# Another order for the paired projection: last two products exchanged, bank sums reordered, row buffers swapped by pair, with row stores, an evacuation and 32 narrow columns moved

## What is computed

```python
def mlstm_project(h, w_in, b_in):
    p = h @ w_in + b_in
    q, k, v, o, gates = jnp.split(p, [hk, 2 * hk, 2 * hk + hv, 2 * hk + 2 * hv], axis=-1)
    ...
# then, per chunk of 128 tokens and in both directions:
#   C_new = a * C + einsum(ws, k, v);  h = (w_inter * q @ C + s @ v) / max(|den|, exp(-m))
```

## Time and profile before

| what | value |
|---|---|
| median of 3 runs | 2076.72 us (2072.17 to 2077.28) |
| profiled execution, its own time | 2077.57 us |
| its span, first to last instruction | 2075.5 us |
| mean granted clock of TensorE | 0.981 of full speed |
| busy: TensorE, its weight loads | 2004.3, 1655.5 us |
| busy: VectorE, GpSimd, ScalarE | 1311.3, 1042.5, 843.7 us |

### The profile page before, as it was taken

The page is one execution under the profiler, slowest core; times in us unless marked ns, Lnnn a source line. Parts: engine busy times, 40 slices in busy tenths (PEclk is TensorE's granted clock), DMA queues, the critical chain, the costliest instruction groups (busy, mean ns, idle before and its releaser), DMA issues.

```text
span 2075.5 us, 24059 instructions
## 1 busy us (share of the span) xinstructions
PE 2004.3 (97%) x9095; PEld 1655.5 (80%) x9095; DVE 1311.3 (63%) x1378; ACT 843.7 (41%) x1118; POOL 1042.5 (50%) x610
## 2 busy tenths in 40 slices
PE   6999999999999999998999999988999999999999
PEld 5788888888788888786787888766788888878877
DVE  6889998877648774975424565589655555523125
ACT  5433356465443222322245464445344334412135
POOL 1376755555212222133474446648877877722254
PEclk7999999999999999999999999999999999999999
DMA  9641112222117543433354765341222222253123
GB/s 377 205 153 41 54 46 74 56 74 70 45 61 267 196 136 89 161 116 100 119 178 142 258 229 163 92 152 61 61 61 62 79 83 86 68 192 125 45 89 127
DMA packets 267920, 248.79 MB, mean 120 GB/s; under 512 B 8266, under 2 KB 229203, under 8 KB 267811
## 3 DMA queue, kind: packets, MB, share of 16 engines
q1 hardware_dynamic: 252243, 229.51, 34.8%
q10 hardware_dynamic: 15568, 17.83, 2.4%
HBM read 203.46 MB, written 43.84 MB: 119 GB/s over the span
## 4 chain that ended last, share of the span: by engine, by line
PE 52%; issue 11%; POOL 6%; DVE 3%; DMA 2%; ACT 1%; SPq 0%; POOLq 0%; DVEq 0%; ACTq 0%
PE PS L2412 16%; PE PS L1902 12%; PE PS L2205 6%; PE PS L2304 5%; PE PS L2175 4%; POOL wl L930 3%; PE PS L2426 1%; PE PS L2248 1%; PE PS L2249 1%; PE PS L2257 1%; PE PS L1932 1%; POOL SCR L1148 1%; PE PS L2091 1%; PE PS L2338 1%; POOL wl L1135 1%
## 5 line engine op out<-in xcount | busy, mean ns | idle before, releaser
L930 POOL TENSOR_TENSOR wl<-raw,wh 128x1024 fp32r<-128x1024 f32 (+1 forms) x145 | 351.2, 2423 | 731.9 <-ACT wh L1204 511.8
L1902 PE MATMUL PS<-XH,wh 128*128 128x512 f32 x1232 | 382.6, 392 | 5.8 <-DVE XL L3263 1.8
L1902 PE MATMUL PS<-XH,wl 128*128 128x512 f32 x1232 | 381.6, 391 | 0.0
L1902 PE MATMUL PS<-XL,wh 128*128 128x512 f32 x1232 | 381.0, 390 | 0.0
L1902 PEld LDWEIGHTS PS<-XH,wh 128*128 128x128 f32 x1232 | 229.3, 188 | 55.1 <-issue 3.0
L1204 ACT ACTIVATE wh<-raw 128x1024 fp32r<-128x1024 f32 (+1 forms) x96 | 98.3, 1024 | 425.0 <-PE PS L1902 141.9
L1902 PEld LDWEIGHTS PS<-XL,wh 128*128 128x128 f32 x1232 | 230.1, 188 | 46.9
L1902 PEld LDWEIGHTS PS<-XH,wl 128*128 128x128 f32 x1232 | 229.8, 188 | 46.6
L2655 DVE SCALAR_TENSOR_TENSOR PS<-B,PJ,PS 128x1022 f32<-128x1022 f32 (+7 forms) x197 | 251.1, 1274 | 7.5
L1277 ACT ACTIVATE wh<-raw 128x1024 fp32r<-128x1024 f32 x48 | 50.8, 1058 | 248.0 <-PE PS L1902 228.6
L1135 POOL TENSOR_TENSOR wl<-SCR,wh 128x512 fp32r<-128x512 f32 x80 | 114.2, 1428 | 69.8 <-ACT wh L1730 69.4
(11 more groups left out here) (487 smaller groups left out, 4252.2 us busy)
## 6 DMA issues: line engine op xcount, KB each, us to landing
raw<-in_ffn_up_w SPq DMA_DIRECT2D x48, 512.0 KB, 4.1
raw<-in_w_in SPq DMA_DIRECT2D x40, 512.0 KB, 4.7
raw<-in_m_in_w SPq DMA_DIRECT2D x37, 512.0 KB, 4.2
SCR<-in_ada_w SPq DMA_DIRECT2D x32, 512.0 KB, 6.7
mod_tiles<-in_mod_w SPq DMA_DIRECT2D x16, 512.0 KB, 13.2
B<-in_ada_w SPq DMA_DIRECT2D x16, 512.0 KB, 4.7
raw<-in_w_out SPq DMA_DIRECT2D x16, 512.0 KB, 4.7
raw<-in_m_out_w SPq DMA_DIRECT2D x16, 512.0 KB, 4.2
```

The source lines that it names most:

```text
L930: tt(wl[slot][:, 0:kc, :], raw[slot][:, 0:kc, :], wh[slot][:, 0:kc, :].bitcast(F32), ALU.subtract).then_inc(lo_done, 1)
L1902: last = mm(ps[:, c:c + step_n], W[:, k, :], Y[:, k, c:c + step_n], start=(seen == 0), stop=(seen == total - 1))
```

## The change

The last two products of each pair are exchanged: products run in the order 0, 1, 2, 3, 4, 6, 5. The seven bank sums follow in the order 1, 4, 3, 6, 3, 2, 5, so that row v is complete after the sixth and row g after the seventh; ScalarE finishes v first and g second. The row buffers change roles from pair to pair. All seven sums of the last pair are made before the recurrence's first key weighting, and TensorE waits for all seven before the first state update. The gate rows are stored after the load of unit 9 instead of unit 7, and SyncE waits for their landing only before it reads them back. VectorE evacuates pass 2 of the value projection before the t3 sums instead of after them. The 32 narrow columns of G2 follow one each behind each wide product instead of two behind each pair.

```diff
@@ o_place, o_out @@
+        O_ORDER = (0, 1, 2, 3, 4, 6, 5)
+        O_SUMS = (1, 4, 3, 6, 3, 2, 5)
+
+        def o_place(q):
+            s, n = divmod(q, 7)
+            return s, O_ORDER[n]
+
-        def o_out(i):
+        def o_out(s, i):
-            return stage[i // 2][:, CTX + HALF * (i % 2):CTX + HALF * (i % 2 + 1)]
+            return stage[(i // 2 + s) % 2][:, CTX + HALF * (i % 2):CTX + HALF * (i % 2 + 1)]
@@ SyncE @@
                 if u in (6, 10, 14):
                     v_store((u - 6) // 4)
-                if u == 7:
+                if u == 9:
                     rows_store()
-                    sp.wait_ge(*at("rows_out", 16 * 10))
...
             for s in range(O_PAIRS):
                 pair_load(s + 1)
                 if s == COLS_AT - 1:
+                    sp.wait_ge(*at("rows_out", 16 * 10))
@@ GpSimd @@
             def o_low(q):
                 pool.wait_ge(*at("oq_hi", q + 1))
-                tt(ring(wl, q), o_weights(q % 7), ring(wh, q).bitcast(F32), ALU.subtract).then_inc(ev("oq_lo"), 1)
+                tt(ring(wl, q), o_weights(o_place(q)[1]), ring(wh, q).bitcast(F32), ALU.subtract).then_inc(ev("oq_lo"), 1)
...
-                pool.wait_ge(*at("oq_lo", 7 * s - 3 + n))
+                if s:
+                    pool.wait_ge(*at("oq_lo", 7 * (s - 1) + O_ORDER.index(3 + n) + 1))
@@ ScalarE @@
             def o_high(q):
-                s, i = divmod(q, 7)
+                s, i = o_place(q)
...
             def o_finish(s, v):
 
-                act.wait_ge(*at("osum_ok", SUMS * s + (4, 7)[v]))
-                row = stage[v][:, CTX:ALL]
+                act.wait_ge(*at("osum_ok", SUMS * s + (7, 6)[v]))
+                row = stage[(v + s) % 2][:, CTX:ALL]
...
-                act.dma_start(...).then_inc(ev(f"proj_out{v}"), 16)
+                act.dma_start(...).then_inc(ev(f"proj_out{(v + s) % 2}"), 16)
...
                 o_copy(s)
                 if s:
-                    o_finish(s - 1, 1)
+                    o_finish(s - 1, 0)
                 o_high(7 * s + 5)
                 o_high(7 * s + 6)
                 if s < O_PAIRS - 1:
-                    for i in range(3):
+                    for i in range(4):
                         o_high(7 * (s + 1) + i)
-                    o_finish(s, 0)
-                    o_high(7 * (s + 1) + 3)
+                    o_finish(s, 1)
...
+            o_finish(O_PAIRS - 1, 1)
             o_finish(O_PAIRS - 1, 0)
-            o_finish(O_PAIRS - 1, 1)
@@ TensorE @@
                         for c in range(0, n, step_n):
                             last = mm(ps[:, c:c + step_n], W[:, k, :], Y[:, k, c:c + step_n], start=(seen == 0), stop=(seen == total - 1))
+                            if single and seen < total - 1:
+                                single(2 * seen + c // step_n)
...
             def late_columns(step_n):
-                if step_n == 6:
+                c = step_n - 10
+                if c == 0:
                     pe.wait_ge(*at("late_summed", LATE * KD))
-                for c in range(max(2 * step_n - 12, 0), min(2 * step_n - 10, LATE * KD)):
+                if 0 <= c < LATE * KD:
                     ins = mm(LATE_PS[:, c:c + 1], late_acc[:, c * P:(c + 1) * P], ones[:], start=True, stop=True)
...
-            group(G2, release="x_used_G2", opened=True, narrow=late_columns)
+            group(G2, release="x_used_G2", opened=True, single=late_columns)
...
             def o_product(s, i):
-                q, (W_H, W_L) = 7 * s + i, (ring(wh, 7 * s + i), ring(wl, 7 * s + i))
-                X_H, X_L = o_tokens(i)
+                q = 7 * s + O_ORDER.index(i)
+                (W_H, W_L), (X_H, X_L) = (ring(wh, q), ring(wl, q)), o_tokens(i)
...
-                    before, n = divmod(earlier[-1], 7)
-                    if n == 0:
+                    before, j = o_place(earlier[-1])
+                    if j == 0:
                         pe.wait_ge(*at("opair_copy", before + 1))
                     else:
-                        pe.wait_ge(*at("osum_ok", SUMS * before + (0, 1, 7, 6, 2, 4, 5)[n]))
+                        pe.wait_ge(*at("osum_ok", SUMS * (before + 1) - O_SUMS[::-1].index(j)))
...
-                for i in range(7):
+                for i in O_ORDER:
                     o_product(s, i)
...
                     if y:
                         pe.wait_ge(*at("p_ok", y))
-                    else:
-                        pe.wait_ge(*at("osum_ok", SUMS * O_PAIRS))
...
                     if x == 0 and h == 0:
-                        pe.wait_ge(*at("osum_ok", SUMS * (O_PAIRS - 1) + 5))
+                        pe.wait_ge(*at("osum_ok", SUMS * O_PAIRS))
@@ VectorE @@
             def bank_sum_pair(s, n):
-                i = (1, 4, 3, 5, 6, 3, 2)[n]
-                dve.wait_ge(*at("oq_used", 7 * s + max(i, (1, 4, 4, 5, 6, 6, 6)[n]) + 1))
+                i = O_SUMS[n]
+                dve.wait_ge(*at("oq_used", 7 * s + max(O_ORDER.index(j) for j in O_SUMS[:n + 1]) + 1))
                 if n == 0:
                     dve.wait_ge(*at("opair_copy", s + 1))
-                    dve.wait_ge(*at("proj_out0", 16 * (DIRECT[0] + s)))
+                    dve.wait_ge(*at(f"proj_out{s % 2}", 16 * (DIRECT[s % 2] + s)))
                 else:
-                    dve.wait_ge(*at("osum_ok", SUMS * s + (0, 1, 2, 3, 3, 5, 5)[n]))
-                if n == 5:
-                    dve.wait_ge(*at("proj_out1", 16 * (DIRECT[1] + s)))
-                g0, g1, v0, v1, u = o_out(0), o_out(1), o_out(2), o_out(3), US[:]
-                dst, src = ((g0, u), (u, u), (g1, u), (g1, g1), (u, u), (v1, u), (v0, u))[n]
-                V.tensor_tensor(dst, o_bank(7 * s + i), src, ALU.add).then_inc(ev("osum_ok"), 1)
+                    dve.wait_ge(*at("osum_ok", SUMS * s + (0, 1, 2, 3, 4, 4, 6)[n]))
+                if n == 4:
+                    dve.wait_ge(*at(f"proj_out{1 - s % 2}", 16 * (DIRECT[1 - s % 2] + s)))
+                g0, g1, v0, v1, u = o_out(s, 0), o_out(s, 1), o_out(s, 2), o_out(s, 3), US[:]
+                dst, src = ((g0, u), (u, u), (g1, u), (u, u), (v1, u), (v0, u), (g1, g1))[n]
+                V.tensor_tensor(dst, o_bank(7 * s + O_ORDER.index(i)), src, ALU.add).then_inc(ev("osum_ok"), 1)
...
             token_low(3 * HK - 1)
+            v_evac(2)
             for k in range(HK):
                 t3_sum(k)
-            v_evac(2)
...
             for s in range(O_PAIRS):
-                for n in range(SUMS if s < O_PAIRS - 1 else 5):
+                for n in range(SUMS):
                     bank_sum_pair(s, n)
...
-                if x == 0:
-                    for h in range(5, SUMS):
-                        bank_sum_pair(O_PAIRS - 1, h)
```

More of the change, by code:

```diff
@@ L1560, in o_finish @@
                     step.link(f(row, row, ACT.Copy, scale=pcol("m_norm_g_2", t)))
-                act.dma_start(qkvo_d[NC:NCH, :, c, :].rearrange("c p t -> p c t"), row.rearrange("p (c t) -> p c t", t=P)).then_inc(ev(f"proj_out{v}"), 16)
+                act.dma_start(qkvo_d[NC:NCH, :, c, :].rearrange("c p t -> p c t"), row.rearrange("p (c t) -> p c t", t=P)).then_inc(ev(f"proj_out{(v + s) % 2}"), 16)
             for q in range(4):
@@ L1890, in _, with product @@
             mm = nc.tensor.matmul
-            def product(ps, w, kc, X, n, ready=None, before=0, release=None, narrow=None):
+            def product(ps, w, kc, X, n, ready=None, before=0, release=None, narrow=None, single=None):
                 XHt, XLt = X
@@ L1940, in tiles, with group @@
                         tile(2 * i + (g.U + s), (g.U + s) % 2, PS[b], taken[b], i + (g.T + s) // 2, **kw)
-            def group(g, ready=None, before=0, release=None, kc=KD, opened=False, narrow=None):
+            def group(g, ready=None, before=0, release=None, kc=KD, opened=False, single=None):
                 def nth_tile(t, i, **kw):
@@ L1954, in group @@
                 nth_tile(g.n - 2, 0)
-                nth_tile(g.n - 1, 0, release=release, narrow=narrow)
+                nth_tile(g.n - 1, 0, release=release, single=single)
             def stat(ps, *srcs, event):
```

## The result

| | before | after |
|---|---|---|
| median of 12 runs | 2078.02 us (2072.17 to 2083.07) | 2064.25 us (2057.89 to 2073.8) |
| profiled execution, its own time | 2077.57 | 2067.65 |
| its span | 2075.5 | 2065.9 |
| mean granted clock | 0.981 | 0.984 |

The ratio is 0.9938 [0.9924, 0.9952]: faster by 0.6%. The forecast was 2063.8 in a range of 2059.5 to 2070.

What follows compares the result with a forecast made beforehand. TensorE, busy for 97% of the span, was taken as the bound. -3.55 - 1.72 - 7.03 - 1.66 + 0.8 + 0.2 = -13.0 gave 2064.6 us, 2063.8 for the median, range 2059.5 to 2070.

Steps and rivals of the forecast that it cites:

- First wait: Value projection, unit 8: moving row stores and SyncE's wait removes 3.55 us of TensorE idling and 1.72 of low clock.
- the row stores still hold the weights: Rival: stores land after 953.4, ScalarE is late for unit 10 and the first wait moves there; 2069 us, chance 0.04.
- Second wait: Value projection, block 18: evacuating before the t3 sums removes 7.03 us of TensorE idling and 1.66 of low clock.
- the evacuation comes late again: Rival: VectorE's operations stretch beside GpSimd and the second wait returns; 2072.5 us wholly, 2069 halfway; chance 0.07.
- Product 6 first, sums and buffers: Pairs: exchanged products, reordered sums and buffers cost 0, with 5.1 us cover for tokens and 3.7 for sums.
- The slower rival: Pairs: a store over 10 us to land, then some 8 us more, makes a bank late; 2082 us, chance 0.02.
- Start of the recurrence: Both remaining bank sums ahead of the first key weighting start the updates about 0.8 us later; bounds 0 and 1.3.
- Columns: G2: one narrow column behind each wide product costs the same, 0.234 us each; the first, earlier one adds 0.2 us.
- The sum: All terms together: -13.0 us against the profiled 2077.57, giving 2064.6, and 2063.8 for the median.

Runs made afterwards that it cites:

- e2: Changed kernel with the row stores after unit 7's load and SyncE's wait for their landing before unit 8's load again: 2068.26 us, ratio 0.9965.
- e1: Changed kernel with the evacuation of pass 2 behind the t3 sums again: 2076.68 us, ratio 0.9993.
- e7: Changed kernel with row v of a pair finished and stored some 4 us later, right ahead of row g's finish: 2066.1 us in one run.
- e8: Changed kernel with the 32 narrow columns two behind each pair of wide products again: 2066.31 us in one run.
- e9: Kernel before with the row-store, SyncE-wait and evacuation moves alone, plus chunk 3's loads taken apart, second direction's first: 2066.62 us, ratio 0.9935.
- e6: Changed kernel with two of the four t3 sums ahead of the evacuation of pass 2: 2065.16 us in one run.
- e11: Changed kernel with the row stores, SyncE's wait and the evacuation of pass 2 as in the kernel before: 2080.89 us, ratio 1.0012.
- e10: Changed kernel with last two bank sums behind first key weighting, context chunk 1's exponentials before last row finishes, readout's first weight parts one chunk later: 2062.7 us, 0.9910.
- e5: Changed kernel with the last two bank sums behind the first key weighting and context chunk 1's exponentials ahead of the last row finishes: 2064.14 us, 0.9938.
- e4: Changed kernel with the last two bank sums of the last pair behind the first key weighting again: 2065.2 us, 0.9955.

## Why the prediction was right, point by point

- **First wait, -3.55 and -1.72.** Right. e2 gives back 5.0 of 5.27. The rival "the row stores still hold the weights" did not come: the load behind the stores left at 944.34, and no wait stands at unit 10.
- **Second wait, -7.03 and -1.66.** Right, a little small: e1 gives back 9.3 of 8.69. Both together gave 13.95 where 13.96 was forecast. The rival "the evacuation comes late again" did not come: bank 10 is the first of the three evacuations that begin at 972.36 and are all done at 974.2, and it is needed at 975.87 + 0.45 = 976.3.
- **Product 6 first, sums and buffers, 0.** The price was right: 114.9 to 115.0 us for the pairs in every run but e7. One step of its working failed: "the next is due when the fifth product ends, 1124.8: 3.7 us of cover", taken from the last pair. In the third pair the first sum waited 11.32 us, and VectorE then stood idle for only 1.84 us before the next. The stores' landings ran to 10.1 us, not 6.5. So the cover in that pair was 1.84 us and not 3.7, and that no cost came is owed to what lies behind it, not to this step. What protects TensorE is the slack behind the sums, which the same paragraph named ("a bank is used again eight products on"): e7 shows that a wait of 12.88 us reaches no bank.
- **The slower rival (row store sets the pair)** was not seen: one landing reached the 10 us that it asked for (10.1, changed kernel), the first sum waited up to 12.88 us in e7, and no bank was late. A store later still was not tried.
- **Start of the recurrence, +0.8.** Right for what it priced (0.96 measured). "As VectorE and TensorE take turns there, nothing takes it back" held too: chunk 3's load is issued at +17.06 instead of +16.10. What the step left out is the wait for that load, which is next in line: 0.8 more until TensorE resumes and 1.65 of clock in the profiled execution. The clock fell there in the changed kernel, e1, e8 and e9, and not in the kernel before or any other run. e1, e6, e7 and e8 have the changed kernel's start of the recurrence to a few hundredths of a microsecond, and TensorE resumed in them at +24.9, +24.0, +24.4 and +24.6 us where the changed kernel has +24.75: in e6 and e7 the chunk loop took 96.2 and 96.6 us, 0.9 and 1.3 more than before the change. So of the 3.3 us some 1.0 is the change's, and the rest comes and goes between executions of the same start. Whether the change makes it more likely is not shown. The step also left out that the longer first wait can itself be followed by a low clock: 2.38 us where it was 1.14, with a fall behind it in e2 and e11 and none in the changed kernel, e1, e6, e7 and e8.
- **Columns, 0, first one +0.2.** Right: 0.227 us each against 0.234. The first one cost 0.4, twice what was forecast, with 0.25 of it as a wait. The Trainium skill's picture (TensorE: Matmul & The Clock Gate, "Part 2: What happens when you issue a matmul") read as one more hidden load per switch would have made the changed kernel's 17 steps 1.9 us shorter; they were 0.4 longer, so the measurement decides against that reading.
- **The sum.** -13.0 forecast, -13.8 by the medians of 12 runs each (2064.25 - 2078.02). The profiled executions differ by 9.9: 13.95 in the projection, less 0.45 ahead of it and 3.3 in the chunk loop, is 10.2, and 0.3 to 0.6 more is lost outside. The interval of the ratio leaves 10.0 to 15.8 us for the gain, so that 13.8 lies this near to 13.0 is in part luck. The start of the projection alone, behind code that the moves don't touch, lies between 884.2 (e10) and 892.7 us (changed) in the profiled executions. Low clock behind waits is a part of this: around 530 us the same wait of 1.83 to 1.86 us was followed by a granted clock of 0.50 in eleven profiles and of 1.00 in three (e2, e7, e10). This is why the medians of many runs, not two profiles, are held against the sum.

What stays open: what sets the time that chunk 3's load takes from issue to use (6.6 to 8.2 us), and what decides whether the clock falls behind a wait of 1.6 to 3.8 us.

## What to carry to other kernels

When a change has many parts, price each against the waits that bound TensorE in the trace: here two moved lines in the order of SyncE and VectorE carried 14 us, and some dozens of changed lines of the pair scheme carried none that could be measured; no wait of TensorE stood in the pairs. A term found as "idle time plus low clock behind it" came out here to within 0.3 and 0.6 us, for waits of 3.2 and 6.9 us; behind shorter waits the clock part came in some runs and not in others. Look also at the next wait downstream of a small delay: 2.5 us more were lost there in the profiled execution.

## What I had not expected

- **The same wait may or may not bring the clock down.** After 2.76 us of idle time (e6) and 2.75 (e5) the granted clock stayed at 1.00, after 2.74 (changed), 2.62 (e8) and 3.20 (e9) it fell. Over all 14 profiles, from 60 us on, falls stand behind waits from 1.64 us up (in e10 also behind two of 0.99 and 0.77 us close together, which e4 and e5 have too, without a fall), and waits without a fall go up to 3.73 us (e1, 1433 us), where the clock fell in all 13 other profiles at this place, with waits of 3.52 to 3.76. So between these the length of the wait alone does not decide. Behind each of the 14 waits of 4.27 us and the three of 6.87 the clock fell. The windows of e5, behind its wait for chunk 3's load, then of e8, then the wait and window of e1:

```profile
1136.70:1139.20 2.50, 2.50 (x19) 1.00 1.04 410
```
```profile
1140.50:1143.00 2.50, 2.24 (x12) 0.64 1.06 409
```
```profile
1433.19 0.47 PE L2420 MATMUL PS<-XH,wh 128*128 128x512 f32 x1 [3.73 <-DVE XL L3210]
```
```profile
1433.20:1435.20 2.00, 2.00 (x9) 1.00 0.57 164
```

- **Some row stores of ScalarE's queue land late.** 3.2 us at the least, median 3.8, 10.1 at the most in the changed kernel (3.2, 3.5 and 6.5 before), with VectorE waiting 41.1 us for them in five waits, and TensorE had no wait in the pairs. What made the late ones late was not asked.
